# Copies of the weight sums issued by ScalarE's queue behind roundings, and the adds, the first blocks' low parts and the final norm placed anew

## The chip, the cores and the metric

One core of a Trainium2 chip runs the kernel. The metric is the device time of one execution in microseconds (us). "Round" in what follows always means: split a float32 into a high part that the matrix unit takes exactly and a low part, the rest; three matmuls (high by high, high by low, low by high) then give nearly the float32 product.

## The reference

Two transformer blocks follow each other on one sequence of 512 tokens of width 1024, all in float32. Cut to what matters:

```python
# first block
h = rmsnorm(x, g_pre);  proj = h @ w_in
att_a = dsa_branch(...)      # indexer scores, top 128 causal keys per query, softmax, 8 heads of 64
att_b = fox_branch(...)      # causal softmax with a forgetting bias, 8 heads of 64
y_a = (att_a * silu(gate_a)) @ w_branch_a;  y_b = (att_b * silu(gate_b)) @ w_branch_b
out = (m_a * y_a + m_b * y_b) @ w_out       # m_a, m_b = sigmoid(h @ w_merge)
x = x + rmsnorm(out, g_post)
x = x + rmsnorm(sigmoid(x @ w_ple_gate) * (p @ w_ple), g_ple)
# second block
h = rmsnorm_2(x, mix_norm_g);  proj = h @ w_in_2
o_a = swa_sink_attention(...)   # window 128, 8 heads, 2 kv heads
o_b = mla_attention(...)        # low-rank q and kv, causal, 8 heads
y = sigmoid(g_a) * (o_a @ w_o_swa) + sigmoid(g_b) * (o_b @ w_o_mla)
x = x + y @ w_out_2
h = rmsnorm_2(x, ffn_norm_g)
x = x + (silu(h @ w_gate) * (h @ w_up)) @ w_down      # d_ff = 2816
return rmsnorm_2(x, final_norm_g)
```

## The kernel before

The activations stay in SBUF; all weights stream through it once. Up to the feed-forward part they come as 67 chunks of up to 128 x 2048 numbers (1 MB), numbered 0 to 66, in two buffers: SyncE issues the load of a chunk, ScalarE writes its high part (`w_hi`, `hi_through`), GpSimd (or, for eight chunks, VectorE) the low part (`w_lo`, `lo_through`), TensorE multiplies. The units in order are, with their chunks: index and value projections and the gates 0 to 14, merge gates `m0` to `m3` 15 to 22, `ya`, `yb` 23 to 26, `wo` 27 to 30, `e`, `pg` 31 to 35, the second block's projections 36 to 42 and 47 to 50, `n0` to `n3` 43 to 46, 51 and 52, `za`, `zb` 55 to 58, `wp` 59 to 62, and the first gate and up weights `f0`, `f1` 63 to 66.

Between these stand four attention stages of 32 units each (a unit is one head by one block of 128 queries): `fox` (some 118 to 190 us), `dsa`, `swa` and `mla`. In each, VectorE and ScalarE make a unit's softmax, GpSimd scales its rows (`scale_rows`, one instruction for each unit), and TensorE turns them, multiplies by V, and fills up with matmuls of the chunks at hand. In `fox` SyncE also moves each head's operands from one place of SBUF to another: six moves of 128 KB and one load of 256 KB for each of heads 2 to 7 (`stack_head`, `load_cum`), when the buffer of the head two before is free, in the same first-in-first-out queue as the loads.

The feed-forward part (from 881 us) uses a Strassen-like scheme of seven products, for which sums of blocks of the gate, up and down weights are formed in DRAM by transfers alone while all else runs. Eight steps of four sums each (`SUM_STEPS`, five for gate and up, three for down) give 32 sums. A sum is a copy from DRAM to DRAM (`copy_for_sum`, 1 MB or less) and then a DMA that adds a second block to it (`add_sum`); the add of a step waits for all four copies of the step (`sum_copied`), and two of the four adds wait for another add. SyncE issues the copies, each behind the load of a chunk (the table `COPY_AFTER`), and GpSimd the adds, each behind the low part of a chunk (`ADD_AFTER`). No add stands in an attention stage.

The feed-forward part begins with `START`: operands of the activations (`t_hi` by ScalarE, `t_lo` by VectorE), and the first seven weight blocks of 128 x 1024, whose low parts GpSimd makes (L977); from block 7 on VectorE makes them (L2023, `block_low`). The `down` part has 20 steps, 0 to 19 (`down_high`, `last_high` on ScalarE, `down_low`, `last_low` on VectorE). The final norm of the four token tiles is the `fin_` functions: those of tiles 0 and 1 stand ahead of step 19 on ScalarE (L1426 to L1442) and VectorE, those of tiles 2 and 3 behind it. What sets the order on each engine is the order in which the code is written; semaphores tie the engines together.

Of the kernel before, what the change touches and what calls it, by code (L numbers as in the profile page):

```python
# [263 lines left out]
COPY_AFTER = (7, 8, 9, 10, 11, 12, 13, 14, 15, 16, 17, 18, 19, 20, 21, 22, 23, 24, 25, 26, 27, 28, 29, 30, 31, 33, 34, 35, 36, 38, 39, 40)  # L264
ADD_AFTER = (15, 16, 19, 20, 21, 22, 23, 24, 25, 26, 27, 28, 29, 30, 31, 33, 34, 35, 36, 39, 40, 43, 55, 56, 57, 58, 59, 60, 61, 62, 63, 64)
# [71 lines left out]
def build(nc, dram, out):  # L337
    ctx = ExitStack()
    with ctx:
# [369 lines left out]
        def _(sp_):  # L709
# [50 lines left out]
            def copy_for_sum(m):  # L760

                table, c0, n = SUM_STEPS[m // 4]
                to, given, _, _ = table[m % 4]
                sp_.dma_start(given_or_sum((SUM, to), table, c0, n),
                              given_or_sum((GIVEN, given), table, c0, n)).then_inc(sum_copied[m // 4], 16)

            for c in range(2, len(CHUNKS)):
                load(c)
                if c in COPY_AFTER:
                    copy_for_sum(COPY_AFTER.index(c))  # L770
# [93 lines left out]
        def _(pool):  # L864
# [3 lines left out]

            def lo_through(c_end):
                for c in range(next_chunk[0], min(c_end + 1, len(CHUNKS))):  # L870
# [20 lines left out]
                    if c in ADD_AFTER:  # L891
                        add_sum(ADD_AFTER.index(c))

# [19 lines left out]
            def scale_rows(name, sc_):  # L913

                a = ATT[name]
                for i in range(NU):
# [4 lines left out]
                    pool.tensor_scalar(s, s, rsum[:, i:i + 1], 1.0, ALU.mult, ALU.mult).then_inc(scaled, 1)  # L921
                    if name == "fox" and i in PAIR_LO_AT:
                        split_pair(PAIR_LO_AT[i])
# [24 lines left out]
            def add_sum(m):  # L948

                table, c0, n = SUM_STEPS[m // 4]  # L950
                to, _, kind, other = table[m % 4]
                pool.wait_ge(sum_copied[m // 4], 64)
                if kind == SUM:
                    pool.wait_ge(sum_added[m % 4 - 2 if m % 4 == 2 else 2], 16 * (m // 4 + 1))
                pool.dma_start(given_or_sum((SUM, to), table, c0, n), given_or_sum((kind, other), table, c0, n),
                               accum_op=ALU.add).then_inc(sum_added[m % 4], 16)

# [16 lines left out]
            lo_through(len(CHUNKS) - 1)  # L974
            for n in range(7):
                pool.wait_ge(block_hi, n + 1)
                pool.tensor_tensor(out=block_of(w_lo, n), in0=block_of(w_raw, n), in1=block_of(w_hi, n).bitcast(F32),  # L977
                                   op=ALU.subtract).then_inc(block_lo, 1)
# [3 lines left out]
        def _(act):  # L982
            nxt = [2]

            def hi_through(c_end):

                for c in range(nxt[0], min(c_end + 1, len(CHUNKS))):
                    n = CHUNKS[c][0] * CHUNKS[c][1]
                    act.wait_ge(w_landed[c % 2], landed[c])
                    if c >= 2:  # L990
                        wait_used(act, c - 2)
                    act.activation(w_hi[:, c % 2, 0:n], w_raw[:, c % 2, 0:n], ACT.Copy).then_inc(w_hi_ready, 1)  # L992
                    nxt[0] = c + 1

# [22 lines left out]
            def hi_half(c, q):  # L1017
# [7 lines left out]
                if q == 1:  # L1025
                    ins.then_inc(w_hi_ready, 1)
                    nxt[0] = c + 1
                elif c in BY_DVE:
                    ins.then_inc(first_half_hi, 1)
# [392 lines left out]
            def fin_square(n, half):  # L1422

                b = (n + 2) % NB
                act.wait_ge(fin_sum, 2 * n + half + 1)
                act.activation(sq[:, half, :], xr[:, b, S * half:S * half + S], ACT.Square,  # L1426
                               accum_out=qs[:, half, b:b + 1]).then_inc(fin_sq, 1)

            def fin_root(n):

                b = (n + 2) % NB
                act.wait_ge(fin_bias, n + 1)
                act.wait_ge(fin_sq, 2 * n + 2)
                act.activation(rT[:, b:b + 1], qs[:, 1, b:b + 1], ACT.Sqrt, scale=1.0 / D,
                               bias=qs[:, 0, 4 + b:5 + b]).then_inc(fin_rms, 1)

            def fin_first_half(n):

                b = (n + 2) % NB
                act.wait_ge(fin_inv, n + 1)  # L1440
                act.wait_ge(fin_ready, n + 1)
                act.activation(xr[:, b, 0:S], xr[:, b, 0:S], ACT.Copy, scale=qs[:, 1, 4 + b:5 + b]).then_inc(half_scaled[0], 1)  # L1442

# [11 lines left out]
            for i in range(4):  # L1455
                t_high(i)
            first_high(0)
            for i in range(4, 7):
                t_high(i)
            block_high(0)  # L1460
            block_high(1)
            silu(1)
            block_high(2)
            for f in range(START, PAIRS):
                n = 7 * (f - START)
                block_high(n + 3)
                block_high(n + 4)
                for g in range(2):
# [8 lines left out]
                block_high(n + 5)  # L1477
# [15 lines left out]
            for d in range(3, STEPS):  # L1493
                if d == STEPS - 1:
                    for n in range(2):
                        fin_square(n, 0)
                        fin_square(n, 1)
                        fin_root(n)
                        fin_first_half(n)
# [9 lines left out]
            fin_square(2, 0)  # L1509
            fin_square(2, 1)  # L1510
            fin_root(2)
            fin_square(3, 0)
            fin_first_half(2)
            fin_square(3, 1)
            fin_root(3)
            fin_first_half(3)


        @block.vector
        def _(dve):  # L1520
# [530 lines left out]
            def block_low(n):  # L2051

                if 7 <= n < BLOCKS:
                    dve.wait_ge(block_hi, n + 1)
                    dve.wait_ge(block_lo, n)
# [58 lines left out]
            tell(last, 1)  # L2114
            b11, b12, b21, b22 = (xT[:, a:a + KH, c:c + HT] for a in (0, KH) for c in (0, HT))
# [7 lines left out]
            operands(0, products(0))  # L2123
            t_low(2)
            first_low(0)
            t_low(3)
            gates_out(1, fg, 0)
            for i in range(4, 7):
                t_low(i)
            gates_out(1, fu, 2)  # L2130
            for f in range(START, PAIRS):
# [5 lines left out]
                made = products(f - 1)  # L2137
# [5 lines left out]
                operands(f - 1, made)  # L2143
                block_low(n + 5)
                first_low(f - 1)
                block_low(n + 6)
# [27 lines left out]
            low_at, high_at = slice(0, S), slice(S, D)  # L2174

            def fin_add(n, half):

                b, i, at = (n + 2) % NB, n % 2, (low_at, high_at)[half]
                product = "p7" if n < 2 else ("p2", "p3")[half]
                wait_filled(dve, product, i)  # L2180
                (minus if n < 2 and half else plus)(xr[:, b, at], xr[:, b, at], bank_of(product, i)[:]).then_inc(fin_sum, 1)

            def fin_gain(n):

                b = (n + 2) % NB
                dve.wait_ge(fin_sq, 2 * n + 1)
                dve.tensor_scalar(qs[:, 0, 4 + b:5 + b], qs[:, 0, b:b + 1], 1.0 / D, EPS,
                                  ALU.mult, ALU.add).then_inc(fin_bias, 1)
                mult(xr[:, b, low_at], xr[:, b, low_at], gfin[:, low_at]).then_inc(fin_ready, 1)

# [529 lines left out]
```

## Time and profile before

| | |
|---|---|
| median of 3 runs | 1210.23 us (1209.99 to 1212.33) |
| the profiled execution | 1208.32 us, of which the span is 1206.5 us |
| granted TensorE clock, mean | 0.99 |
| TensorE busy (matmul) | 1166.1 us, 97% of the span |
| VectorE, ScalarE, GpSimd busy | 819.9, 630.9, 411.5 us |
| DMA | 216.30 MB, mean 179 GB/s |
| adds (software queue) | 4608 packets, 30.41 MB |

An engine's busy time counts its instructions' durations once; what is left of the span is idle. "Waits" list what ended each idle time; "issue" is a wait that the profile ties to nothing. A DMA's "us to landing" runs from its issue to its completion. The granted clock 1.0 is 2.4 GHz and 0.5 is 1.2 GHz: a window's value between them is the mean.

### The profile page before, as it was taken

To read this page: it belongs to the slowest core of one execution; us is meant where nothing else is said; L and a number is where in the kernel's file an instruction comes from. 1 tells how busy PE (TensorE), PEld (TensorE's weight loads), DVE (VectorE), ACT (ScalarE), POOL (GpSimd) and SP (SyncE) were. 2 spreads that over 40 slices of the span, in tenths; PEclk is the share of its full clock that TensorE was granted. 3 is DMA by queue.
4 is the path that set the end of the run, shared out by engine and by line. 5 is a ranking of instruction groups with operands and counts; after the bars stand their busy time and mean duration, and the time that the engine had idled before them with its cause. 6 is when DMAs were issued, how large, how long until landed. Compare 5 with 4: busy or idle time off the path is not lost.

```text
span 1206.5 us, 17475 instructions
## 1 busy us (share of the span) xinstructions
PE 1166.1 (97%) x6392; PEld 1000.5 (83%) x6392; DVE 819.9 (68%) x1663; ACT 630.9 (52%) x1105; POOL 411.5 (34%) x287
## 2 busy tenths in 40 slices
PE   9999999999999799999899999899989999999996
PEld 8878778888888687789778788688879999998885
DVE  5789874774628237699981775672599878786575
ACT  6553574476522345448683787333364454544454
POOL 1428462445544334312362676345435000000000
PEclk9999999999999899999999999999999999999998
DMA  8216773713998996555321402787546666667871
GB/s 276 79 63 244 210 244 141 227 53 140 287 274 230 298 280 192 163 207 147 106 39 37 140 1 69 213 208 176 138 156 199 206 204 202 205 218 256 312 261 70
DMA packets 91092, 216.30 MB, mean 179 GB/s; under 512 B 18424, under 2 KB 28152, under 8 KB 83968
## 3 DMA queue, kind: packets, MB, share of 16 engines
q1 hardware_dynamic: 83232, 180.46, 44.6%
q0 software_dynamic: 4608, 30.41, 12.4%
q10 hardware_dynamic: 3168, 4.33, 1.0%
q8 instruction: 51, 0.84, 0.3%
q14 instruction: 33, 0.27, 0.1%
HBM read 198.24 MB, written 71.45 MB: 224 GB/s over the span
## 4 chain that ended last, share of the span: by engine, by line
PE 71%; DVE 15%; DMA 4%; ACT 3%; issue 3%; POOL 2%; SPq 0%; ACTq 0%; DVEq 0%; POOLq 0%
PE bank L2302 38%; PE bank L2624 14%; PE bank L2638 8%; PE bank L2366 3%; PE bank L2398 2%; PE bank L2380 2%; PE bank L2444 2%; DVE sc L1789 2%; DMA w_raw<-in_w_out 1%; DVE m L1785 1%; DVE sqS L1935 1%; DMA w_raw<-in_w_o_mla 1%; POOL w_lo L907 1%; DVE t_lo L2023 1%; DMA rot<-in_rot 1%
## 5 line engine op out<-in xcount | busy, mean ns | idle before, releaser
L888 POOL TENSOR_TENSOR w_lo<-w_raw,w_hi 128x2048 fp32r<-128x2048 f32 (+4 forms) x49 | 218.1, 4451 | 366.3 <-ACT w_hi L992 311.8
L2302 PE MATMUL bank<-aH,w_hi 128*128 128x512 f32 x544 | 218.7, 402 | 2.6 <-DVE mqT L1986 1.0
L2302 PE MATMUL bank<-aH,w_lo 128*128 128x512 f32 x544 | 212.4, 391 | 0.0
L2302 PE MATMUL bank<-aL,w_hi 128*128 128x512 f32 x544 | 205.8, 391 | 0.0
L992 ACT ACTIVATE w_hi<-w_raw 128x2048 fp32r<-128x2048 f32 (+4 forms) x45 | 82.9, 1843 | 128.3 <-PE bank L2302 94.9
L2624 PE MATMUL bank<-t_hi,w_hi 128*128 128x256 f32 x504 | 143.5, 285 | 6.0 <-POOL w_lo L977 3.6
L2624 PE MATMUL bank<-t_hi,w_lo 128*128 128x256 f32 x504 | 143.1, 284 | 0.0
L2624 PE MATMUL bank<-t_lo,w_hi 128*128 128x256 f32 x504 | 143.1, 284 | 0.0
L2302 PEld LDWEIGHTS bank<-aH,w_hi 128*128 128x128 f32 x544 | 102.6, 189 | 22.2 <-issue 4.4
L2302 PEld LDWEIGHTS bank<-aL,w_hi 128*128 128x128 f32 x544 | 102.1, 188 | 22.3
L2302 PEld LDWEIGHTS bank<-aH,w_lo 128*128 128x128 f32 x544 | 102.5, 188 | 16.3
L2023 DVE TENSOR_TENSOR w_lo<-w_raw,w_hi 128x1024 fp32r<-128x1024 f32 (+2 forms) x69 | 96.5, 1398 | 27.3 <-ACT w_hi L1414 21.3
L1394 ACT ACTIVATE w_hi<-w_raw 128x1024 fp32r<-128x1024 f32 x63 | 66.5, 1060 | 81.5 <-PE bank L2624 81.5
L2624 PEld LDWEIGHTS bank<-t_hi,w_hi 128*128 128x128 f32 x504 | 97.4, 193 | 6.7 <-POOL w_lo L977 4.0
L2624 PEld LDWEIGHTS bank<-t_hi,w_lo 128*128 128x128 f32 x504 | 97.4, 193 | 0.0
L2624 PEld LDWEIGHTS bank<-t_lo,w_hi 128*128 128x128 f32 x504 | 97.3, 193 | 0.0
L2302 PE MATMUL bank<-uH,w_hi 128*128 128x512 f32 x192 | 75.4, 393 | 4.1 <-DVE uL L2007 4.1
L2302 PE MATMUL bank<-uL,w_hi 128*128 128x512 f32 x192 | 75.4, 393 | 0.0
L2302 PE MATMUL bank<-uH,w_lo 128*128 128x512 f32 x192 | 75.3, 392 | 0.0
L1638 DVE TENSOR_TENSOR pT<-bank,pT 128x256 fp32r<-128x256 f32 (+3 forms) x128 | 58.3, 457 | 12.8 <-ACT pT L1066 12.8
L1066 ACT ACTIVATE pT<-bank 128x256 fp32r<-128x256 f32 (+3 forms) x128 | 52.7, 412 | 25.5 <-PE bank L2380 24.2
L2302 PE MATMUL bank<-w_hi,aH 128*128 128x512 f32 (+4 forms) x192 | 64.3, 335 | 0.0
(414 smaller groups left out, 2687.2 us busy)
## 6 DMA issues: line engine op xcount, KB each, us to landing
w_raw<-in_w_in SPq DMA_DIRECT2D x21, 1024.0 KB, 5.0
w_raw<-up_sums SPq DMA_DIRECT2D x36, 512.0 KB, 4.3
w_raw<-in_gate_up SPq DMA_DIRECT2D x35, 512.0 KB, 4.2
up_sums<-in_gate_up SPq DMA_DIRECT2D x16, 1024.0 KB, 7.8
w_raw<-in_w_merge SPq DMA_DIRECT2D x8, 1024.0 KB, 5.0
up_sums<-in_gate_up POOLq DMA_DIRECT2D x8, 1024.0 KB, 11.6
up_sums<-up_sums POOLq DMA_DIRECT2D x8, 1024.0 KB, 10.8
w_raw<-in_w_out SPq DMA_DIRECT2D x8, 1024.0 KB, 7.3
```

Of the source, the lines that this page charges most:

```text
L888: pool.tensor_tensor(out=w_lo[:, c % 2, 0:n], in0=w_raw[:, c % 2, 0:n], in1=w_hi[:, c % 2, 0:n].bitcast(F32), op=ALU.subtract).then_inc(w_ ...
L992: act.activation(w_hi[:, c % 2, 0:n], w_raw[:, c % 2, 0:n], ACT.Copy).then_inc(w_hi_ready, 1)
L1066: act.activation(p_views(a, u, pt, 0), t_view(a, u), ACT.Copy).then_inc(p_hi, 1)
L1394: act.activation(block_of(w_hi, n), block_of(w_raw, n), ACT.Copy).then_inc(block_hi, 1)
L1638: empties(dve.tensor_tensor(out=p_views(a, u, pt, 1), in0=t_view(a, u), in1=p_views(a, u, pt, 0).bitcast(F32), op=ALU.subtract), name + ". ...
L1789: ins = dve.match_replace(out=sc[:, lo:hi], in_to_replace=m8[:, b - 1, :], in_values=sc[:, lo:hi], imm_value=TAKEN)
L2023: return dve.tensor_tensor(out=o, in0=a, in1=b, op=ALU.subtract)
L2302: ins = pe.matmul(o, l, r, start=(kk == 0 and operand == ROUNDED and m == 0), stop=(kk == total - 1 and operand == REST), skip_group_check ...
L2366: ins = pe.matmul(o, q, k, start=(m == 0), stop=(m == len(pairs) - 1))
L2380: ins = pe.transpose(o[:, at * P:(at + 1) * P], src, ident[:])
L2624: ins = pe.matmul(o, l[:, k, col], r[:, k, :], start=(i < 4 and k == 0 and m == 0), stop=(i >= 2 and k == KH - 1 and m == 2), skip_group_c ...
L2638: ins = pe.matmul(bank_of(name, i)[:], l, r, start=start and m == 0, stop=stop and m == 2, skip_group_check=True)
```

## The change

The two tables are new. The copies are issued by ScalarE's queue, each behind the rounding of a chunk; the adds may also stand behind a scaling of an attention unit.

```diff
-COPY_AFTER = (7, 8, 9, 10, 11, 12, 13, 14, 15, 16, 17, 18, 19, 20, 21, 22, 23, 24, 25, 26, 27, 28, 29, 30, 31, 33, 34, 35, 36, 38, 39, 40)
-ADD_AFTER = (15, 16, 19, 20, 21, 22, 23, 24, 25, 26, 27, 28, 29, 30, 31, 33, 34, 35, 36, 39, 40, 43, 55, 56, 57, 58, 59, 60, 61, 62, 63, 64)
+COPY_AFTER = (3, 4, 5, 6, 6, 6, 8, 9, 10, 12, 13, 14, 15, 16, 16, 16, 16, 17, 18, 19, 21, 22, 23, 24, 45, 45, 45, 47, 49, 51, 52, 52)
+ADD_AFTER = (7, 8, 9, ("fox", 6), ("fox", 12), ("fox", 18), ("fox", 24), ("fox", 30), 15, 16, ("dsa", 6), ("dsa", 12),
+             ("dsa", 18), ("dsa", 24), ("dsa", 30), 19, 20, 21, 22, 23, 24, 25, 26, 33,
+             51, 52, ("mla", 2), ("mla", 7), ("mla", 12), ("mla", 17), ("mla", 22), 59)
...
             for c in range(2, len(CHUNKS)):
                 load(c)
-                if c in COPY_AFTER:
-                    copy_for_sum(COPY_AFTER.index(c))
...
+            def adds_after(place_):
+
+                if place_ in ADD_AFTER:
+                    add_sum(ADD_AFTER.index(place_))
...
                     pool.tensor_scalar(s, s, rsum[:, i:i + 1], 1.0, ALU.mult, ALU.mult).then_inc(scaled, 1)
+                    adds_after((name, i))
...
-            lo_through(len(CHUNKS) - 1)
-            for n in range(7):
-                pool.wait_ge(block_hi, n + 1)
-                pool.tensor_tensor(out=block_of(w_lo, n), in0=block_of(w_raw, n), in1=block_of(w_hi, n).bitcast(F32),
-                                   op=ALU.subtract).then_inc(block_lo, 1)
+            lo_through(len(CHUNKS) - 2)
...
+            def copy_for_sum(m):
+
+                table, c0, n = SUM_STEPS[m // 4]
+                to, given, _, _ = table[m % 4]
+                act.dma_start(given_or_sum((SUM, to), table, c0, n),
+                              given_or_sum((GIVEN, given), table, c0, n)).then_inc(sum_copied[m // 4], 16)
...
                     act.activation(w_hi[:, c % 2, 0:n], w_raw[:, c % 2, 0:n], ACT.Copy).then_inc(w_hi_ready, 1)
                     nxt[0] = c + 1
+                    copies_after(c)
...
             for d in range(3, STEPS):
-                if d == STEPS - 1:
-                    for n in range(2):
-                        fin_square(n, 0)
-                        fin_square(n, 1)
-                        fin_root(n)
-                        fin_first_half(n)
                 down_high(d)
...
-                if 7 <= n < BLOCKS:
+                if n < BLOCKS:
                     dve.wait_ge(block_hi, n + 1)
-                    dve.wait_ge(block_lo, n)
                     minus(block_of(w_lo, n), block_of(w_raw, n), block_of(w_hi, n).bitcast(F32)).then_inc(block_lo, 1)
...
+            minus(w_lo[:, (n_chunks - 1) % 2, :], w_raw[:, (n_chunks - 1) % 2, :],
+                  w_hi[:, (n_chunks - 1) % 2, :].bitcast(F32)).then_inc(w_lo_ready, 1)
...
+            fin_add(0)
+            fin_add(1)
+            fin_gain(0)
+            fin_scale(0)
```

The rest of the diff writes the same `fin_` work in one loop over the tiles behind the last step, and moves `block_high`, `t_high`, `block_low`, `t_low` and the first products within `START`. TensorE's own order of instructions is the same in both.

GpSimd, around the start of `fox`, before (`w_lo` is a chunk's low part, `sp` the softmax rows, `qbT` and `kbT` the head operands):

```order
L888 TENSOR_TENSOR w_lo<-w_raw,w_hi 128x2048
L936 TENSOR_TENSOR qbT<-qbT,oddQ 128x512
L936 TENSOR_TENSOR kbT<-kbT,oddK 128x512
L921 TENSOR_SCALAR sp<-sp,rsum 128x128
L921 TENSOR_SCALAR sp<-sp,rsum 128x256
L921 TENSOR_SCALAR sp<-sp,rsum 128x384
L921 TENSOR_SCALAR sp<-sp,rsum 128x512
L921 TENSOR_SCALAR sp<-sp,rsum 128x128
L921 TENSOR_SCALAR sp<-sp,rsum 128x256
L921 TENSOR_SCALAR sp<-sp,rsum 128x384
L936 TENSOR_TENSOR qbT<-qbT,tQ 128x512
```

After:

```order
L896 TENSOR_TENSOR w_lo<-w_raw,w_hi 128x2048
L869 DMA up_sums<-up_sums 128x2048
L944 TENSOR_TENSOR qbT<-qbT,oddQ 128x512
L944 TENSOR_TENSOR kbT<-kbT,oddK 128x512
L928 TENSOR_SCALAR sp<-sp,rsum 128x128
L928 TENSOR_SCALAR sp<-sp,rsum 128x256
L928 TENSOR_SCALAR sp<-sp,rsum 128x384
L928 TENSOR_SCALAR sp<-sp,rsum 128x512
L928 TENSOR_SCALAR sp<-sp,rsum 128x128
L928 TENSOR_SCALAR sp<-sp,rsum 128x256
L928 TENSOR_SCALAR sp<-sp,rsum 128x384
L869 DMA up_sums<-up_sums 128x2048
```

An add (the DMA rows) now stands behind the low part of chunk 9, as behind those of 7 and 8, and one behind the seventh scaling; there are five within `fox`, six units apart, where none stood.

VectorE in `START` (`t_lo` an activation operand, `w_lo` a weight block, `uu` and `held` the first products' operands), before:

```order
L2023 TENSOR_TENSOR t_lo<-xT,t_hi 128x1024
L2023 TENSOR_TENSOR t_lo<-t_raw,t_hi 128x1024
L2023 TENSOR_TENSOR t_lo<-xT,t_hi 128x1024
L1535 TENSOR_TENSOR fu<-bank,rB 128x512 x2
L1535 TENSOR_TENSOR sq<-fg,fu 128x512
L1535 TENSOR_TENSOR held<-fg,fu 128x256
L1535 TENSOR_TENSOR sq<-fg,fu 128x256
L2023 TENSOR_TENSOR uu<-fm,bank 128x256 x2
L2023 TENSOR_TENSOR held<-sq 128x256
L2023 TENSOR_TENSOR sq<-sq 128x256 x2
L2026 TENSOR_TENSOR held<-held,sq 128x256
L2023 TENSOR_TENSOR first_lo<-sq,first_hi 128x1024
```

After:

```order
L2013 TENSOR_TENSOR w_lo<-w_raw,w_hi 128x1024 x2
L2013 TENSOR_TENSOR t_lo<-t_raw,t_hi 128x1024
L2013 TENSOR_TENSOR t_lo<-xT,t_hi 128x1024
L2013 TENSOR_TENSOR w_lo<-w_raw,w_hi 128x1024
L2013 TENSOR_TENSOR uu<-fm,bank 128x256 x2
L2013 TENSOR_TENSOR w_lo<-w_raw,w_hi 128x1024
L1525 TENSOR_TENSOR sq<-fg,fu 128x512
L1525 TENSOR_TENSOR held<-fg,fu 128x256
L1525 TENSOR_TENSOR sq<-fg,fu 128x256
L2013 TENSOR_TENSOR held<-sq 128x256
L2013 TENSOR_TENSOR sq<-sq 128x256 x2
L2016 TENSOR_TENSOR held<-held,sq 128x256
```

The `w_lo` rows of blocks 0 to 6, which GpSimd had, stand among VectorE's, and the two `uu` rows now stand ahead of the products' (`sq`, `held`).

ScalarE at the end of the down part (`w_hi` and `last_hi` step 19's operands, the `xr` and `sq` rows the final norm), before:

```order
L1402 ACTIVATE last_hi<-last_from 128x1024
L1426 ACTIVATE sq,qs<-xr 128x512 x2
L1434 ACT_TABLE_LOAD
L1434 ACTIVATE rT<-qs 128x1
L1442 ACTIVATE xr<-xr,qs 128x512
L1426 ACTIVATE sq,qs<-xr 128x512 x2
L1434 ACTIVATE rT<-qs 128x1
L1442 ACTIVATE xr<-xr,qs 128x512
L1414 ACTIVATE w_hi<-w_raw 128x1024
L1402 ACTIVATE last_hi<-last_from 128x512
```

After:

```order
L1411 ACTIVATE last_hi<-last_from 128x1024
L1423 ACTIVATE w_hi<-w_raw 128x1024
L1411 ACTIVATE last_hi<-last_from 128x512
L1498 ACTIVATE sq,qs<-xr 128x512 x2
L1502 ACT_TABLE_LOAD
L1502 ACTIVATE rT<-qs 128x1
L1506 ACTIVATE xr<-xr,qs 128x512
L1498 ACTIVATE sq,qs<-xr 128x512 x2
L1502 ACTIVATE rT<-qs 128x1
```

Step 19's two roundings now stand ahead of the final norm of tiles 0 and 1.

## Rows read from the trace of the kernel before

**Rows 1.** The page: busy time, share and instructions.

```profile
PE 1166.1 (97%) x6392; PEld 1000.5 (83%) x6392; DVE 819.9 (68%) x1663; ACT 630.9 (52%) x1105; POOL 411.5 (34%) x287
```

**Rows 2.** Waits of TensorE, whole span: us in total, times, longest.

```profile
PE bank L2302 <- issue: 7.1, 3, 6.4
PE bank L2302 <- DVE uL L2007: 4.1, 1, 4.1
PE bank L2638 <- DVE last_lo L2023: 4.1, 1, 4.1
PE bank L2624 <- POOL w_lo L977: 3.6, 1, 3.6
...
PE bank L2380 <- POOL sc L921: 1.9, 5, 0.5
...
PE bank L2624 <- DVE vv L2026: 1.6, 1, 1.6
```

**Rows 3.** Windows: length, busy time by engine, granted clock, DMA share, GB/s.

```profile
414.00:422.00 8.00, 3.45 (x9) 2.84 (x10) 5.63 (x4) 5.86 (x9) 5.20 (x2) 0.57 0.73 274
773.00:777.00 4.00, 4.00 (x12) 2.64 (x11) 4.00 (x8) 2.71 (x4) 0.00 (x0) 0.57 1.05 294
902.00:907.00 5.00, 3.69 (x20) 3.69 (x21) 5.00 (x2) 1.99 (x3) 5.00 (x3) 0.66 0.35 105
1189.00:1197.00 8.00, 5.97 (x15) 4.72 (x16) 3.01 (x4) 1.27 (x4) 0.00 (x0) 0.57 0.17 64
```

**Rows 4.** DMA issues of 393 to 394.6 us: count, KB each, us to landing.

```profile
xT<-in_xT SPq DMA_DIRECT2D x1, 2048.0 KB, 11.0
w_raw<-in_w_out SPq DMA_DIRECT2D x1, 1024.0 KB, 18.1
```

**Rows 5.** DMA issues of 750 to 751 us.

```profile
w_raw<-in_w_o_mla SPq DMA_DIRECT2D x1, 1024.0 KB, 14.9
```

**Rows 6.** GpSimd from 898 us: start, duration, [idle before it].

```profile
900.19 20.16 POOL L977 TENSOR_TENSOR w_lo<-w_raw,w_hi 128x1024 fp32r<-128x1024 f32 x7 [17.01 <-ACT w_hi L1394]
```

**Rows 7.** VectorE, 898 to 926 us.

```profile
904.27 3.39 DVE L2023 TENSOR_TENSOR t_lo<-xT,t_hi 128x1024 fp32r<-128x1024 f32 x1
...
922.67 1.22 DVE L2023 TENSOR_TENSOR first_lo<-sq,first_hi 128x1024 fp32r<-128x1024 f32 x1 [1.12 <-ACT first_hi L1376]
```

**Rows 8.** ScalarE, 1179 to 1192 us.

```profile
1180.78 0.63 ACT L1426 ACTIVATE sq<-xr 128x512 f32<-128x512 f32 x1 [3.15 <-DVE xr L2026]
...
1187.99 1.04 ACT L1414 ACTIVATE w_hi<-w_raw 128x1024 fp32r<-128x1024 f32 x1
```

**Rows 9.** VectorE and TensorE near the end.

```profile
1200.20 0.39 PE L2638 MATMUL bank<-w_hi,last_lo 128*128 128x512 f32 x1
...
1202.69 0.75 DVE L2198 SCALAR_TENSOR_TENSOR xr<-xr,qs,gfin 128x512 f32<-128x512 f32 x1
```

**Rows 10.** Waits of TensorE, 118 to 240 us.

```profile
PE bank L2366 <- DMA fK<-kbT: 0.5, 1, 0.5
```

**Rows 11.** SyncE queue: the last move of a head.

```profile
148.04 0.60 SPq L748 DMA_DIRECT2D fK<-kbT  x1
```

**Rows 12.** DMA issues of 147.2 to 148.2 us.

```profile
fK<-kbT SPq DMA_DIRECT2D x2, 128.0 KB, 2.6
```

**Rows 13.** TensorE: the first matmul of that head.

```profile
151.57 0.39 PE L2366 MATMUL bank<-fK,fQ 128*128 128x128 f32 x2
```

**Rows 14.** DMA issues of 219.9 to 221 us: an add and a load.

```profile
w_raw<-in_w_merge SPq DMA_DIRECT2D x1, 1024.0 KB, 4.9
```

**Rows 15.** DMA issues of 234.3 to 235.5 us, the same two.

```profile
up_sums<-in_gate_up POOLq DMA_DIRECT2D x1, 1024.0 KB, 12.0
w_raw<-in_w_merge SPq DMA_DIRECT2D x1, 1024.0 KB, 8.4
```

**Rows 16.** GpSimd's adds, whole span: duration ns; then idle before them.

```profile
L955 POOL DMA_DIRECT2D up_sums<-up_sums x10: 802/824/846, 300.5 to 539.9; - x10
...
  issue: 20.5, 9
```

## What the change does to the time

> **What bounds the kernel now.** I read the page first. TensorE is busy for 1166.1 us of 1206.5 (97%) [rows 1], so all that another engine can give back is TensorE's idle 40.4 us and what a lowered clock costs. Then the waits of TensorE [rows 2], to see whether that idle time is many small waits or few large ones: four single waits hold 18.2 us (6.4, 4.1, 4.1 and 3.6 us), and a fifth 1.6 us. Then windows around them for the granted clock [rows 3]: it is 0.57 as a mean of 414 to 422 us, of 773 to 777 and of 1189 to 1197, so behind these waits TensorE works for a time at 1.2 GHz and not at 2.4. The change touches what stands behind each of the four. Last I looked at what it puts into places that have no wait today, the attention stages.
>
> **Part 1: the 6.4 us at 412 us.** TensorE waits for the second chunk of `wo`. Its load landed 18.1 us after its issue, behind a 2 MB activation load that took 11.0 us, and with copies and adds of sums in flight [rows 4]. A 1 MB load with an add that has just been issued beside it takes 4.9 us [rows 14]. In the new tables no copy stands between chunks 24 and 45 and no add between 26 and 33. So the 2 MB and the 1 MB run alone. Without the sums they take no longer than 11.0 + 4.9 = 15.9 us by these rows. A move of 128 KB lands in 2.6 us [rows 12] and the 1 MB load in 4.9, so 0.875 MB cost 2.3 us and 3 MB some 2.6 + 2.875 x 2.63 = 10.2 us. I take this one: the chunk lands 8 us earlier and the whole 6.4 us goes; with 15.9 only 2.2 us go, which is the other end. Behind the wait the low clock (0.57 over 8 us is 6.9 us at half) lies on all but the last 0.5 us of the window's 3.45 us of work [rows 3], which, at twice the duration, costs 1.4 us. Part 1: **-7.8** (-2 to -8).
>
> **Part 2: the 4.1 us at 769 us.** TensorE waits for VectorE's `uL`, which waits for `w_o_mla`'s chunk; that took 14.9 us to land [rows 5], with adds in flight. The last add now stands behind chunk 59, five behind units of `mla`, done by about 730 us. Mean clock 0.57 over 4 us of unbroken work [rows 3] costs 0.43 x 4 = 1.7 us. Part 2: **-5.8** (-2 to -6).
>
> **Part 3: the start of the feed-forward part.** GpSimd's seven low parts take 20.16 us from 900.19 [rows 6], 2.9 us each. VectorE's `t_lo` of 1.22 us takes 3.39 us while they run [rows 7]. On VectorE the same seven cost 7 x 1.22 = 8.5 us plus one of 2048 columns at about 2.3, and everything else there falls back to its short time. TensorE waits here for GpSimd 3.6 us, `vv` 1.6 us [rows 2] and `fu` 0.7 us, and 1.4 us go to the clock (0.66 as a mean of 902 to 907 [rows 3]): 7.3 us in all. VectorE's new order needs its 10.8 us of low parts earlier; walking it through with the short durations leaves about 1.1 us of waiting. Part 3: **-6.2** (-3 to -7.3). What is late next is `vv`.
> The Trainium skill (SBUF — State Buffer, its part on engine ports) calls the port pair that VectorE and GpSimd share an exclusive lock held for a whole instruction; 3.39 us where 1.22 was needed fits that better than a fair share, which would give about 2.4.
>
> **Part 4: the end.** ScalarE squares tile 0 from 1180.78, having waited 3.15 us, and rounds step 19's chunk only at 1187.99 [rows 8]; TensorE waits 4.1 us for `last_lo` [rows 2] and then works at half clock: 0.57 over 8 us is 6.9 us, less the 2.0 us of the window that were idle, is 4.8 us of work at twice its duration, 2.4 us lost [rows 3]. Put ahead, step 19's four roundings (1.04 us for the first [rows 8], 3.5 in all) are done by 1183, before TensorE needs them at 1186.98. The price is that the norm of tiles 0 and 1 (8 us of a chain between two engines) now runs beside these last matmuls, and those of 2 and 3 behind it. In before the last scale ended 1202.69 + 0.75 = 1203.44, 2.8 us behind TensorE's end (1200.20 + 0.39) [rows 9]; I estimate 4.1. Part 4: -4.1 - 2.4 + 1.3 = **-5.2** (-3 to -6.5).
>
> Gains: 7.8 + 5.8 + 6.2 + 5.2 = 25.0 us.
>
> **Part 5: the copies on ScalarE's queue.** An issue takes ScalarE's queue under 1 us and mostly falls beside a running activation; the only dense place is four behind chunk 16, some 2 us, my upper end with 1 us for another place. The copies leave the loads' queue, so a load need not stand behind a copy, but both now run at once. I take 0 (-1 to +3).
> The Trainium skill (DMA: Bandwidth & Descriptors, "Queues, rings and completion order") says each DMA engine goes round-robin between the queues that have work. With load, copy and add in three queues in place of two, a load's share beside both falls from a half to a third. By that the stretch in part 6 would be 7 and not 3.5 us for each head that meets both; three copies stand near `fox`, so the sum would be some 7 us worse (rival B).
>
> **Part 6: adds in `fox`.** This is the largest loss. A head's moves are 6 x 128 KB and 256 KB, 1 MB. They have hardly any slack: head 2's were late by 0.5 us [rows 10], and head 4's last was issued at 148.04 [rows 11], landed 2.6 us later [rows 12] at 150.64, and TensorE used it at 151.57 [rows 13]: 0.9 us. What an add does to 1 MB in SyncE's queue the two loads show: 4.9 us where the add was issued 0.1 us before [rows 14] but its data came later, 8.4 us in the other case [rows 15]: up to 3.5 us more. No add lies in `fox` now; five will, and two or three more right before, each 8 to 12 us in flight, so nearly every one of heads 2 to 7 meets one. Six heads x (3.5 - 0.9) = 15.6 us if each is hit in full; a head's moves are spread over 4 us and many a packet is past before, so half is my middle, 8; one more for copies behind chunks 8 to 10 in the third queue: **+9** (0 to +16).
>
> **Part 7: adds in `dsa` and `mla`.** No head moves there; the loads have slack. An add costs GpSimd 0.8 us between scalings, and TensorE waits for these already 1.9 us in five times [rows 2]. Ten adds x 0.8 = 8 us at most; half is hidden: **+4** (0 to +10), which holds an add that waits for another add's landing.
>
> **Sum.** -25 + 0 + 9 + 4 = -12 on 1208.32 gives 1196.3. The runs' median is 1.9 us above the profiled execution: **1198 us**, its own range 1191 to 1204.
>
> **Rivals.**
> *A. The adds cost nearly nothing.* For it: the 4.9 us case, and part 6's slack applies only while the data flow. Against it: 0.5 us of wait exists already. Then 1208.3 - 25 + 3 = 1186, as runs 1188.
> *B. Only a part of the four waits goes*, with the lower ends: -2 - 2 - 3 - 3 = -10, perhaps -17 with one of them full: 1208.3 - 17 + 13 = 1204, as runs 1206. Against: the copies and adds are gone from those places. The same time comes out if the gains are whole but load, copy and add, now in three queues, share the DMA engines evenly: part 6's 3.5 us become 7 for the two heads that copies behind chunks 9 and 10 meet: 1196.3 + 7 = 1203, as runs 1205. Against: a copy's data flow for a few us only. I count the two together.
> *C. Slower: GpSimd stands behind its adds.* Adds don't overlap: of the twenty, nine waited, 20.5 us in all, for nothing that the profile names [rows 16], and one takes 12.0 us to land beside other traffic [rows 15]. Six units of `fox` are about 12 us. If an add in an attention stage takes longer than its six (in `mla` five) units, the next one holds GpSimd's queue with all the scalings behind it, softmax rows come late, and TensorE stalls, then at a low clock too (a wait of 3.6 us and more was always followed by one). It decides from 14 us in flight, which copies beside it may make: 15 adds x 2 us = 30, plus part 6's 9: 1208.3 - 25 + 32 and more = 1216, as runs 1218. Against: taken beside a load and a copy they stay at 12.
> **Chances.** The forecast 0.53, A 0.18, B 0.15, C 0.12, others 0.02. A measurement here tells a difference of 0.2% (2.4 us) from none. Faster than 1207.8: the forecast and A whole, two thirds of B, some 0.82. Within: 0.05. Slower than 1212.7: C and a little, 0.13. The range takes in A and most of B: 1187 to 1210.
>
> **What would show it.** In the profile after: no wait over 1 us at 412, at 769 and at 1187 us and a clock of 1.0 there; VectorE's `t_lo` all at 1.22 us and no wait for GpSimd behind 881 us (parts 1 to 4). In `fox`, waits of TensorE for `fK` of 1 to 4 us, five or so, 9 us in sum, with GpSimd's waits small (part 6). Were these waits instead for GpSimd's scalings, with GpSimd idle before an add, it is C; were there none, A. The forecast is wrong if `wo`'s chunk still lands over 15 us after issue, or if the clock in the attention stages falls.

## The result and the profile after

The changed kernel takes **1223.53 us** in the median of four runs (1222.29 to 1225.24), before 1210.5 us: a ratio of 1.0114, 95% interval [1.0094, 1.0134]. It is slower by 13 us, where 1198 us and a gain were forecast. The profiled execution took 1225.24 us with a span of 1223.4. It is the slowest of the four, and the profiled one before, 1208.32 us, lies below all of its runs, so the two traces lie 16.9 us apart where the medians lie 13.0.

The page after answers to [rows 1]: TensorE's busy time rose by 5.3 us for the same instructions in the same order, so a part of the loss is clock; its idle time rose by 11.6 us, to 52.0. In the slices the clock dips in the sixth, 153 to 184 us, which is in `fox`. The queues: q0 is the software queue of the adds, q10 ScalarE's, which now has the copies' 30 MB (4.33 MB before).

```profile
PE 1171.4 (96%) x6392; PEld 1004.0 (82%) x6392; DVE 812.5 (66%) x1671; ACT 631.9 (52%) x1105; POOL 387.7 (32%) x279
...
PEclk9999979999999999999999989999999999999999
...
q0 software_dynamic: 4608, 30.41, 12.9%
q10 hardware_dynamic: 7776, 34.74, 7.7%
```

The waits of TensorE after, in the columns of [rows 2]. The four waits of before are gone (6.4, 4.1, 4.1, 3.6 us, and `vv`'s 1.6); `fK` (an operand of `fox`, moved by SyncE) has 16.0 us where it had 0.5 [rows 10], and two new large rows name GpSimd: `mK`, an operand of `mla`, and the scaled rows `sp`, of `dsa` mostly (0.9 us of them in `fox`).

```profile
PE bank L2367 <- DMA fK<-kbT: 16.0, 3, 7.7
PE bank L2367 <- POOL mK L952: 7.6, 2, 6.9
PE bank L2381 <- POOL sp L928: 5.6, 4, 4.0
PE bank L2381 <- POOL sc L928: 2.9, 6, 1.0
...
PE bank L2625 <- DVE fg L1525: 0.9, 1, 0.9
```

The windows of after, in the columns of [rows 3]: three in `fox`, one in `dsa`, one in `mla`, then the places where `wo`, `za` and the end had their waits. The first five have a clock of 0.57 to 0.81, the last three of 1.00.

```profile
132.00:141.00 9.00, 4.49 (x18) 3.33 (x17) 1.81 (x13) 1.47 (x5) 1.77 (x3) 0.81 1.00 291
151.00:166.00 15.00, 7.32 (x29) 5.96 (x30) 2.81 (x12) 3.39 (x10) 1.34 (x3) 0.66 0.63 147
178.00:186.00 8.00, 6.26 (x23) 5.22 (x24) 2.50 (x11) 2.65 (x7) 2.07 (x3) 0.57 0.92 208
273.00:281.00 8.00, 6.33 (x22) 5.60 (x23) 1.37 (x6) 2.19 (x6) 2.96 (x5) 0.57 0.72 137
714.00:722.00 8.00, 5.37 (x20) 4.54 (x21) 1.31 (x9) 1.24 (x5) 4.29 (x6) 0.57 0.83 199
414.00:446.00 32.00, 32.00 (x143) 26.50 (x142) 17.59 (x18) 13.11 (x17) 12.98 (x3) 1.00 0.50 169
770.00:810.00 40.00, 39.76 (x183) 32.53 (x182) 21.86 (x26) 22.93 (x36) 13.92 (x6) 1.00 0.36 132
1189.00:1197.00 8.00, 8.00 (x37) 6.64 (x36) 7.65 (x8) 4.01 (x4) 0.00 (x0) 1.00 0.85 289
```

Both kernels run the same TensorE instructions in the same order, so the difference between the starts of one instruction in the two traces, its lag, says where the time went. It changes at eight places; the first seven are waits, with the low clock around them:

| place | lag before it, us | after it | change | forecast |
|---|---|---|---|---|
| `fox`, three waits for `fK` | 0.2 | 24.1 | +23.9 | +9 |
| `dsa`, one wait for `sp`, small ones | 24.1 | 31.5 | +7.4 | +4 with `mla` |
| `wo`, second chunk (412 us before) | 31.5 | 23.5 | -8.0 | -7.8 |
| `mla`, waits for `mK` and `sc` | 23.5 | 35.4 | +11.9 | (above) |
| `za` (769 us before) | 35.4 | 30.1 | -5.3 | -5.8 |
| start of the feed-forward part | 30.1 | 23.4 | -6.7 | -6.2 |
| the last step | 23.4 | 16.6 | -6.8 | -6.5 |
| the final norm behind it | 16.6 | 16.9 | +0.3 | +1.3 |

Gains of 26.8 us and losses of 43.5, with the 0.2 us that stood there at the start, make the span's 16.9. The gains came as forecast; what failed is the price of the adds in the attention stages and just ahead of them. For `wo`, the second chunk's load, issued at 425.38 us, landed after 10.4 us where it was 18.1, close to the 10.2 that part 1 took:

```profile
w_raw<-in_w_out SPq DMA_DIRECT2D x1, 1024.0 KB, 10.4
```

The three waits in `fox` are those of heads 1, 3 and 5 (4.5, 7.7 and 3.9 us). Head 3's last moves now look like this. The last was issued at 148.14 us, in 0.60 us as in [rows 11]; the two moves named `fK<-kbT` took 10.8 us to land where it was 2.6 [rows 12]. The add beside them was issued at 146.17.

```profile
up_sums<-up_sums POOLq DMA_DIRECT2D x1, 1024.0 KB, 12.4
...
fK<-kbT SPq DMA_DIRECT2D x2, 128.0 KB, 10.8
```

In the six microseconds from 149 to 155 us the DMA engines gave 87% of their time to the add (q0) and 5.7% to the moves (q1): 99 packets of 8 KB and 62 of mostly 2 KB:

```profile
q0 software_dynamic: 99, 0.81, 87.2%
q1 hardware_dynamic: 62, 0.11, 5.7%
```

In the one microsecond from 157 to 158, with the add nearly through, 166 packets of q1 passed:

```profile
q1 hardware_dynamic: 166, 0.28, 90.2%
```

In `dsa` GpSimd stood in front of an add, the one behind unit 6. The columns are start, duration and, in brackets, the idle time before. The add before it was issued at 258.57 and took 14.1 us, so it landed at 272.7; the next was issued at 273.03, and the scaling `sp` behind it, for which TensorE waited 4.0 us, came then.

```profile
up_sums<-in_gate_up POOLq DMA_DIRECT2D x1, 1024.0 KB, 14.1
```

```profile
258.57 0.83 POOL L869 DMA_DIRECT2D up_sums<-in_gate_up  x1
...
273.03 0.85 POOL L869 DMA_DIRECT2D up_sums<-up_sums  x1 [5.61 <-issue]
273.64 1.76 POOL L928 TENSOR_SCALAR sp<-sp,rsum 128x512 f32<-128x512 f32 x3
```

The same before `mla`: the add behind chunk 51 was issued at 699.02 and took 13.8 us; the one behind chunk 52 had to wait for its landing, and `mK` of head 1, which TensorE wanted at 709.72, came behind.

```profile
down_sums<-in_down POOLq DMA_DIRECT2D x1, 1024.0 KB, 13.8
```

```profile
699.02 0.85 POOL L869 DMA_DIRECT2D down_sums<-in_down  x1
...
713.13 0.83 POOL L869 DMA_DIRECT2D down_sums<-in_down  x1 [5.89 <-issue]
...
715.32 1.25 POOL L952 TENSOR_TENSOR mK<-mkT,mK 64x512 fp32r<-64x512 f32 x1
```

### The profile page after: what moved, and what is told of

Its sections match the earlier page's. It is cut to its first block, busy times and chain, and to the rows that moved or that the text cites. A ratio compares the mean times of both kernels' runs of the same rounds, so it can differ in the third digit from the quotient of the medians.

```text
span 1223.4 us, 17419 instructions
## 1 busy us (share of the span) xinstructions
PE 1171.4 (96%) x6392; PEld 1004.0 (82%) x6392; DVE 812.5 (66%) x1671; ACT 631.9 (52%) x1105; POOL 387.7 (32%) x279
## 4 chain that ended last, share of the span: by engine, by line
PE 73%; DVE 11%; POOL 4%; issue 4%; DMA 3%; ACT 2%; SPq 1%; ACTq 0%; DVEq 0%; POOLq 0%
PE bank L2303 41%; PE bank L2625 15%; PE bank L2639 7%; DMA fK<-kbT 3%; PE bank L2399 2%; PE bank L2445 2%; PE bank L2367 2%; PE bank L2381 2%; DVE sqS L1925 1%; DVE sc L1779 1%; DVE m L1775 1%; POOL w_lo L914 1%; POOL w_lo L896 1%; DMA w_raw<-in_w_in 1%; SPq L749 1%
## 5 line engine op out<-in xcount | busy, mean ns | idle before, releaser
L896 POOL TENSOR_TENSOR w_lo<-w_raw,w_hi 128x2048 fp32r<-128x2048 f32 (+4 forms) x48 | 213.9, 4456 | 378.4 <-ACT w_hi L999 324.2
L2303 PE MATMUL bank<-aH,w_hi 128*128 128x512 f32 x544 | 221.3, 407 | 2.9 <-DVE mqT L1976 1.1
L2013 DVE TENSOR_TENSOR w_lo<-w_raw,w_hi 128x1024 fp32r<-128x1024 f32 (+2 forms) x77 | 106.6, 1394 | 27.8 <-ACT w_hi L1423 21.5
## 6 DMA issues: line engine op xcount, KB each, us to landing
up_sums<-in_gate_up POOLq DMA_DIRECT2D x8, 1024.0 KB, 10.9
```

What stands on the lines that cost most here:

```text
L896: pool.tensor_tensor(out=w_lo[:, c % 2, 0:n], in0=w_raw[:, c % 2, 0:n], in1=w_hi[:, c % 2, 0:n].bitcast(F32), op=ALU.subtract).then_inc(w_ ...
L2013: return dve.tensor_tensor(out=o, in0=a, in1=b, op=ALU.subtract)
L2303: ins = pe.matmul(o, l, r, start=(kk == 0 and operand == ROUNDED and m == 0), stop=(kk == total - 1 and operand == REST), skip_group_check ...
```

## The experiments

**e1: the new start and end alone.** Both tables and the copies' queue as before, on the changed kernel:

```diff
-COPY_AFTER = (3, 4, 5, 6, 6, 6, 8, 9, 10, 12, ...)
-ADD_AFTER = (7, 8, 9, ("fox", 6), ...)
+COPY_AFTER = (7, 8, 9, 10, 11, 12, 13, 14, ...)      # as before, behind SyncE's loads
+ADD_AFTER = (15, 16, 19, 20, 21, 22, 23, ...)        # as before
```

> This kernel keeps the transfers of before (both tables, copies on SyncE's queue behind loads) and takes only the new order at the start of the feed-forward part and at the end. Theory: the placing of adds and copies alone made the change slower, and parts 3 and 4 are gains of their own (6.5 and 6.8 us by the lag of TensorE's instructions). Then 1210.5 - 13 = 1197 us, with the 6.4 and 4.1 us waits at 412 and 769 us back and no new wait in fox. Rival: VectorE's extra low parts or the serial norm cost what they gain once the end is not moved by other things: 1208 to 1212.

Measured: 1195.96 us, ratio 0.9894 [0.9879, 0.9909]. The two waits of the transfers are back, `fK` is at 1.2 us, and the rows for `last_lo` and for GpSimd's low parts do not exist any more.

```profile
PE bank L2300 <- issue: 6.2, 3, 5.4
PE bank L2300 <- DVE uL L1994: 4.1, 1, 4.1
...
PE bank L2364 <- DMA fK<-kbT: 1.2, 2, 0.7
```

So parts 3 and 4 gain 13 us by themselves, in the expected 1197 us within 1, and all that made the change slower lies in the tables and the queue: 1223.5 less 1196 leaves 27 us for these, net of the two waits that they remove.

**e2: six adds cut to almost nothing.**

```diff
+TINY = (2, 3, 4, 5, 6, 7)
...
                 table, c0, n = SUM_STEPS[m // 4]
+                n = 16 if m in TINY else n
```

This kernel leaves out most of six sums.

> The changed kernel with the sums' adds 2 to 7 (those behind chunk 9, behind the five units of fox) cut to 16 of their 2048 columns: the rest of these six sums is left out; issues, waits and all copies stay. Theory: the data of the adds alternate with the small packets of the head moves on each DMA engine, and that is most of the 24 us that fox lost; copies are the smaller part. Then the waits for fK fall from 16.0 to under 5 us, with no half clock in fox or once: some 1204 to 1209. Rival (GpSimd stands behind its adds, and the issue itself is the cost): the waits stay, 1220. Rival (the copies, in their own queue now, do it): waits for fK stay over 10 us, 1215 and more.

Measured: 1201.68 us, ratio 0.9937 [0.9923, 0.9952], 22 us below the changed kernel. `fK` falls from 16.0 to 0.7 us; the two waits for GpSimd further on are untouched.

```profile
PE bank L2369 <- POOL mK L954: 7.1, 2, 6.4
PE bank L2383 <- POOL sp L930: 4.9, 4, 3.9
...
PE bank L2369 <- DMA fK<-kbT: 0.7, 2, 0.5
```

It came out below the expected 1204 to 1209, because the copies, which stayed, cost little here: the lag behind `fox` is 2.2 us, where it was 24.1. The issues stayed too, so nearly the whole cost in `fox` goes with the adds' data. A hold of GpSimd would have shrunk with them as well, but TensorE's waits in `fox` name the moves (16.0 us) and hardly GpSimd (0.9 us).

**e4: the copies out of `fox`.**

```diff
-COPY_AFTER = (3, 4, 5, 6, 6, 6, 8, 9, 10, 12, ...)
+COPY_AFTER = (3, 4, 5, 6, 6, 6, 6, 6, 12, 12, ...)
```

> The changed kernel with the copies that stood behind chunks 8, 9 and 10 moved to before (two more behind chunk 6) and behind (chunk 12) fox; all adds stay. Theory (each queue gets its turn by packet, so add and copy each add their own packets' time to a head's moves): the waits for fK for heads 1 and 3, which met both, shrink by 2 to 3 us each, head 5's stays: 1217 to 1220. Rival (only adds matter): 1223. Rival (the copies on ScalarE's queue are the main cost): 1205.

Measured: 1224.85 us, ratio 1.0126 [1.0109, 1.0143]. Waits for `fK` of 6.9 and 3.6 us stay for heads 3 and 5 (7.7 and 3.9 in the changed kernel). Head 1's 4.5 us went, but five copies at one place made a chunk late, a wait of 6.0 us at 112 us (`w_lo`), and TensorE came to head 1 some 8 us later for it, so its case tells nothing of the copies. The total, in which the new wait hides what head 1 gave back, tells little either. From head 3's wait to the end of `fox` the lag grows by 15.5 us, in the changed kernel by 17.1: the theory's 2 to 3 us for head 3 were too much, and for these heads the adds are most of it. With an add alone beside the moves, the window of 151 to 156 us shows the mechanism without a copy in the way: 94 packets of 0.77 MB and 82 of 0.14 MB, nearly as many of one as of the other, and 88% of the engines' time to 8.7%.

```profile
PE bank L2365 <- DMA fK<-kbT: 11.1, 3, 6.9
...
PE bank L2301 <- POOL w_lo L894: 6.5, 3, 6.0
```

```profile
q0 software_dynamic: 94, 0.77, 88.0%
q1 hardware_dynamic: 82, 0.14, 8.7%
```

**e6: the same six adds, half as wide.**

```diff
+TINY = (2, 3, 4, 5, 6, 7)
...
                 table, c0, n = SUM_STEPS[m // 4]
+                n = n // 2 if m in TINY else n
```

It leaves out half of six sums.

> The changed kernel with adds 2 to 7 cut to half their columns (the other half of these six sums is left out): as many packets, each of 4 KB and not 8. Theory (the moves' packets alternate one for one with the add's, so a move pays the add's time per packet): the waits of heads 3 and 5 shrink by the halved packet time, 9 x 0.35 = some 3 us each, to 4 to 5 and under 1; waits for fK 16.0 to 6 or 8 us, and less half clock: 1210 to 1214. Rival (an add costs a fixed time by being in the software queue, whatever its size): 1220 to 1223.

Measured: 1212.16 us, ratio 1.0019 [1.0009, 1.0029], in the expected 1210 to 1214. The waits for `fK` are 10.9 us in five times where they were 16.0 in three. Head by head, 1 fell from 4.5 to 1.5 us and 5 from 3.9 to 0.4, but head 3 only from 7.7 to 6.3, and head 6, which had none, now has 2.5: the add behind unit 18 is issued at 171.29 us, in the middle of its moves. So the waits in sum stand above the expected 6 to 8. Half the data gives back half of what all of it cost (11.4 of 21.9 us), with the clock in it; it does not give back half of each wait. From 143 to 147 us, beside head 3's moves, the add's and the moves' packets are again nearly equal in number. A 4 KB packet of the add took some 0.47 us there (69.0% of 16 engines' 4 us, by 94), an 8 KB one in e4 some 0.75, so half the data is not half the time; the add at 141 us was still 10.6 us in flight. Why so long is open.

```profile
PE bank L2369 <- DMA fK<-kbT: 10.9, 5, 6.3
```

```profile
q0 software_dynamic: 94, 0.36, 69.0%
q1 hardware_dynamic: 91, 0.15, 12.5%
```

```profile
up_sums<-up_sums POOLq DMA_DIRECT2D x1, 512.0 KB, 10.6
```

**e3: no add ahead of `mla`.**

```diff
-             51, 52, ("mla", 2), ("mla", 7), ("mla", 12), ("mla", 17), ("mla", 22), 59)
+             ("mla", 2), ("mla", 7), ("mla", 12), ("mla", 17), ("mla", 22), ("mla", 27), 57, 59)
```

> The changed kernel with the adds that stood behind chunks 51 and 52 moved into mla and behind it (units 2, 7, 12, 17, 22, 27 and chunks 57, 59). Theory: the second of them waited 5.9 us for the first to land, with the operand mK of head 1 queued behind it on GpSimd, and TensorE stood for 6.9 + 0.7 us and then ran at half clock. Then both waits go, and -7.6 - 3.5 of clock - up to 1: 1212 us. Rival: mK is late for another reason (its own rounding by ScalarE): 1222 to 1224.

Measured: 1214.36 us, ratio 1.0041 [1.0026, 1.0056], 9 us less than the changed kernel and 2 above the expected 1212. The row for `mK` is gone, `fK` stays at 16.0 us.

**e8: the add behind chunk 16 cut to almost nothing.**

```diff
+TINY = (9,)
...
                 table, c0, n = SUM_STEPS[m // 4]
+                n = 16 if m in TINY else n
```

It leaves out most of one sum.

> The changed kernel with one add, number 9 (behind chunk 16), cut to 16 of its columns; the rest of that sum is left out. In the changed kernel it was issued at 258.57, landed at 272.71 us beside four copies, and the next add, behind unit 12 of dsa, was held until 273.03 with GpSimd's scalings behind it: TensorE waited 4.0 us and ran at half clock. Theory (an add holds GpSimd until the one before has landed): the wait goes, and 4.0 + up to 3 us of clock with it: 1217 to 1220. Rival (the four copies from ScalarE's queue delay dsa themselves): 1223.

Measured: 1216.81 us, ratio 1.0056 [1.0042, 1.0070], 7 us less, at the lower edge of the expected 1217 to 1220. The next add (behind unit 6 of `dsa`; the expectation has 12 by mistake) is issued 0.16 us after GpSimd is free and not 5.61, and `sp` falls from 5.6 to 1.1 us. The four copies are in both, so the wait was not theirs directly. They do lengthen an add: the one cut to 8 KB still took 8.7 us to land beside them.

```profile
up_sums<-in_gate_up POOLq DMA_DIRECT2D x1, 8.0 KB, 8.7
```

```profile
267.86 0.85 POOL L871 DMA_DIRECT2D up_sums<-up_sums  x1 [0.16 <-issue]
```

**e5: two adds that no semaphore ties together.**

```diff
-ADD_AFTER = (15, 16, 19, 20, 21, 22, ...)     # e1's table
+ADD_AFTER = (15, 16, 19, 20, 22, 22, ...)
```

> e1_start_end_only with the add that stood behind chunk 21 placed with the one behind chunk 22. These two adds have no semaphore that ties them to each other. Theory: the second of two adds on GpSimd's queue is issued only when the first has landed, whatever the program's waits say, so it is issued 0.3 us after the first's landing, 7 to 12 us after the first's issue, and GpSimd is idle between. Rival (the waits seen so far were the program's semaphores): the second is issued within 1 us of the first, and the two are in flight together.

Measured in one run: 1197.11 us. The first add was issued at 332.14 and took 10.8 us, so it landed at 342.9; the second was issued at 343.21, with GpSimd idle for 10.26 us between.

```profile
332.14 0.82 POOL L881 DMA_DIRECT2D up_sums<-in_gate_up  x1
343.21 0.84 POOL L881 DMA_DIRECT2D up_sums<-in_gate_up  x1 [10.26 <-issue]
```

```profile
up_sums<-in_gate_up POOLq DMA_DIRECT2D x1, 1024.0 KB, 10.8
```

An add holds GpSimd's whole queue until the one before has landed, though nothing in the program asks for it; what makes it wait no run shows. That is what the unnamed 20.5 us before adds were [rows 16]: in the kernel before, eight adds with 20.3 us of that idle time ahead of them are issued 0.31 to 0.32 us after the landing of the add before. The adds that were held in `dsa` and ahead of `mla` are not tied to the one before by a semaphore either.

**e7: the copies back on SyncE's queue.**

```diff
             for c in range(2, len(CHUNKS)):
                 load(c)
+                copies_after(c)        # sp_.dma_start; the two calls on ScalarE are taken out
```

> The changed kernel with its 32 copies back on SyncE's queue, each behind the load of the chunk behind whose rounding it stood. Theory: the queue that issues the copies is worth little, since e4 took copies out of fox and gained nothing: 1219 to 1225, with head 1's wait smaller (the copies of chunks 8 to 10 now start before fox). Rival (ScalarE's queue, a third ring, is a main cost): 1205 to 1212.

Measured: 1215.86 us, ratio 1.0057 [1.0038, 1.0076]. That is between the theory's range and the rival's: neither held. The profiled execution, 1220.14 us, is the slowest of the four (the others 1215.2 to 1216.0), so its trace shows 5 of the 8 us only. In it `fox` is unchanged, `mK` and `sp` shrink, and GpSimd's other scaled rows, `sc`, grow from 2.9 to 4.8 us. By the lag it is mostly `dsa` that gives back: +1.8 us where it was +7.4; `mla` has +11.4 where it was +11.9.

```profile
PE bank L2366 <- DMA fK<-kbT: 16.2, 3, 8.2
PE bank L2380 <- POOL sc L942: 4.8, 6, 2.3
PE bank L2366 <- POOL mK L966: 4.2, 2, 3.5
PE bank L2380 <- POOL sp L942: 2.4, 4, 1.2
```

Behind a load a copy starts earlier than behind a rounding: the four behind chunk 16 are issued from 237 us on, not from 252, and have landed by 256 us, before add 9 is issued at 259.5. It lands after 11.4 us and not 14.1, and the next add's hold of GpSimd falls from 5.61 us to 2.87. So the copies behind roundings on ScalarE's queue cost some 8 us by the medians. In `dsa` the way is this: copies beside an add make it land later, and the next one holds GpSimd longer. These microseconds lie inside those that the lag gives to the adds in `dsa` and `mla`, not beside them. That this is the whole of the 8 us is not shown, and as this kernel moves queue and moment together, it does not tell which of the two it is.

**b1 and b2: the gains without the losses.** The new start and end; copies on SyncE's queue; no add in `fox`, `dsa` or `swa`, no copy and no add near `wo`'s chunks, none behind chunks 51, 52 and 55 to 58.

```diff
+COPY_AFTER = (4, 5, 6, ..., 25, 31, 33, 34, 35, 36, 38, 39, 40, 41, 42)
+ADD_AFTER = (7, 8, 13, 15, 16, 19, 20, 21, 22, 23, 24, 25, 26, 31, 33, 34, 35, 36, 39, 40, 43,
+             47, 49, ("mla", 7), ("mla", 12), ("mla", 17), ("mla", 22), 59, 60, 61, 62, 63)      # b1
+             ("mla", 2), ("mla", 7), ("mla", 12), ("mla", 17), ("mla", 22), ("mla", 27), 59, ...)  # b2
```

> The new start and end with tables that put no add into fox, dsa or swa, none and no copy near the second chunk of wo, none behind chunks 51, 52 and 55 to 58, four into mla; copies on SyncE's queue. Theory: e1's 1196 less the whole wait and low clock at 412 us (7.8) and at 769 us (5.4): 1183 us, with no wait of TensorE over 2.5 us. Rival (each add moved makes a wait elsewhere): 1190 or more.

Measured: 1187.96 us, ratio 0.9820 [0.9805, 0.9834], where 1183 was expected. Most of it, but a new wait of 4.0 us for a chunk's low part stood behind the add of chunk 49.

```profile
PE bank L2300 <- POOL w_lo L908: 4.2, 2, 4.0
```

> b1_sums_apart with the two adds behind chunks 47 and 49 moved to units 2 and 27 of mla. In b1 the one behind 49 was issued at 656.17 us and TensorE then waited 4.0 us at 668 us for the low part of a chunk, and ran at half clock. Theory: that wait was the add's doing (traffic beside the loads): 1188 - 4.0 - 1.5 = 1182 to 1184. Rival: six adds in mla cost what they save, 1187 to 1190.

Measured: **1183.49 us**, ratio 0.9785 [0.9772, 0.9798]: 27 us below the kernel before and 40 below the changed one, in the expected 1182 to 1184. That wait is gone.

```profile
PE bank L2300 <- POOL w_lo L908: 0.2, 1, 0.2
```

## Why the prediction was wrong

Parts 1 to 4 were right, each within 1.3 us of its term, and e1 confirms 3 and 4 on their own (13 us); b2, which has all four, is 27 us below before. The largest difference is in part 4: the norm behind the last step cost 0.3 us where 1.3 were taken. VectorE's `t_lo` is at 1.22 us throughout, now that GpSimd does not work beside it, as part 3 had it. It named `vv` as late next; what is late is `fg`, with 0.9 us.

```profile
918.97 1.22 DVE L2013 TENSOR_TENSOR t_lo<-t_raw,t_hi 128x1024 fp32r<-128x1024 f32 x1
```

Parts 6 and 7 failed, and each is half of the error: 14.9 and 15.3 us more than their terms. The prediction had named the sign of it, a clock that falls in the attention stages.

**Part 6**: +9 was forecast, +23.9 came, above its upper end of 16. Two things in it were wrong. First, its price for a head. The 3.5 us of [rows 15] came from a load that was nearly through when the add's data began: from 234 to 239 us 466 packets of its queue had passed, some nine tenths of its 1 MB.

```profile
q1 hardware_dynamic: 466, 0.95, 55.8%
```

From 239 to 242 us what was left of it went at the add's pace, 66 packets of that queue to 63 of the add. So the trace of before had the mechanism in it, beside the very load that the price was read from.

```profile
q0 software_dynamic: 63, 0.52, 83.0%
q1 hardware_dynamic: 66, 0.14, 13.5%
```

While an add's data flow, packets of 2 KB pass about one for each of its 8 KB packets (99 to 62, 94 to 82, 63 to 66), and a head whose moves are under way can lose most of the add's data time: `fK<-kbT` took 8.2 us more, not 3.5. This is in line with the rule of the Trainium skill (DMA: Bandwidth & Descriptors, "Queues, rings and completion order") that was cited and used only for the third queue, where e4 shows that it was worth little; that page puts some 9 to 17 descriptors into a packet, and whether the profile's packet is the same thing no run here shows. The number of heads came out right: half of six at the full price is three heads, and three were hit. What each of the three waited was 5.3 us in the mean, where 3.5 - 0.9 = 2.6 were taken. Why the others were spared is not shown; e6, where head 6 waits and head 5 hardly does, suggests that it hangs on when an add falls.

Second, the clock behind the waits was put at nothing, without a reason, although the four waits of before had each been followed by half clock [rows 3]. The waits in `fox` are 16.0 + 0.9 us; the other 7 us of its 23.9 are matmuls at 1.2 GHz, in windows of 0.81, 0.66 and 0.57.

**Part 7 failed by its form.** It counted 0.8 us for each of ten adds' issue, and not the two behind chunks 51 and 52, just ahead of `mla`. What cost was rival C's mechanism: an add holds GpSimd until the last one has landed. C set its point of decision at 14 us in flight; the adds beside copies and loads took 13.8 and 14.1 us (above). But the two adds that held GpSimd came up only 8 and 9 us after the one before them was issued, since that one stood behind a chunk and not six units back, which C had not looked at. 4.0 and 6.9 us of wait and the half clock behind them make 19.3 us with the small waits, where 4 were forecast and 10 were the upper end. C's time, 1218 us, was near by luck: its 30 us lay on fifteen adds, and two did it; and with part 6's 9 its own terms make 39 us, not the 32 of its sum, and 1224 us as runs.

**Part 5** gave the copies on ScalarE 0 (-1 to +3). e7 has them at some 8 us, above that range, by a way that the sum did not hold: through the adds.

The chance of 0.13 for slower was too low. The full price for each of the six heads would not have shown it: with 16 us in place of 9 the sum is 1205 us as runs, still a gain. It took the clock behind the waits and the hold of GpSimd, and both stood in rows of before [rows 3, 16].

## What to carry over

Price a new transfer beside small-packet transfers by its own data time, not by bytes shared: each small packet may wait for a large one, and a stage whose transfers land just in time pays it in full, then again in clock. When such a price is read off a row, look how much of the transfer was still to come when the other's data began. Don't put an accumulating DMA on GpSimd's queue ahead of work that another engine awaits, unless the one before it has landed by then. Where a change gains in some places and loses in others, align the two traces by the bound engine's instructions: the lag shows each term of the sum.

## What the runs showed of the hardware

- Adds on the software queue do not overlap: the second of two was issued 0.3 us after the first landed, GpSimd idle for 10.26 us, with no semaphore between them (e5).
- While an add's 8 KB packets flow, about as many 2 KB packets of another queue pass: 94 of the add to 82 of the moves in 5 us, and 88% of the time to 8.7% (e4); 63 to 66 beside a load (before); with packets of 4 KB 94 to 91 (e6).
- Every TensorE wait of 3.5 us or more in these traces came with a stretch at 1.2 GHz, of 3.4 to 10.2 us, that began during the wait or up to 0.8 us behind it. Of shorter waits some did: the wait of 2.3 us for `skS` was followed by one of 3.4 us in b2 and by none in the kernel before.
